# Mixture-of-experts loop: rows sorted once ahead of it, 32 rows always and 64 more if needed, narrow and wide jobs in turn

## The reference, cut to what matters

```python
def grouped_moe(x, w_router, router_bias, w_gate, w_up, w_down):
    scores = jax.nn.sigmoid((x @ w_router).astype(jnp.float32))
    sel = scores + router_bias.astype(jnp.float32)
    ...                       # one group of four experts, then its two best
    combine = ...             # normalised gates, 0 for experts not chosen
    y = jnp.zeros_like(x)
    for e in range(N_EXPERTS):
        h = jax.nn.silu(x @ w_gate[e]) * (x @ w_up[e])
        y = y + combine[..., e:e + 1] * (h @ w_down[e])
    return y
```

## Time and profile before

| what | value |
|---|---|
| median of 3 runs (lowest, highest) | 1649.84 us (1643.22, 1656.58) |
| the profiled execution, its own time | 1639.89 us |
| its span in the trace | 1637.9 us |
| mean granted TensorE clock | 0.971 of 2.4 GHz |
| PE busy | 1497.6 us (91%) |
| DVE, ACT, POOL busy | 435.7, 253.6, 160.7 us |
| bytes moved | 558.64 MB, 341 GB/s over the span |

### The profile page before, as it was taken

The page is one execution under the profiler, slowest core; times in us unless marked ns, Lnnn a source line. Parts: engine busy times, 40 slices in busy tenths (PEclk is TensorE's granted clock), DMA queues, the critical chain, the costliest instruction groups (busy, mean ns, idle before and its releaser), DMA issues.

```text
span 1637.9 us, 18866 instructions
## 1 busy us (share of the span) xinstructions
PE 1497.6 (91%) x7398; PEld 678.2 (41%) x7399; DVE 435.7 (27%) x765; ACT 253.6 (15%) x546; POOL 160.7 (10%) x157
## 2 busy tenths in 40 slices
PE   4899936998999889999899998999999999999995
PEld 3566413554445424434244342443434434434442
DVE  3103947776560402010220102201022012011014
ACT  3001031232100122101121011210112102102201
POOL 0101983121220000000000000000000000000001
PEclk9999967999999999999999999999999999999998
DMA  9998245776795699997799976999789999999993
GB/s 385 404 377 322 73 171 181 267 263 252 279 363 212 245 398 421 421 403 290 282 421 422 406 289 266 423 422 413 294 325 422 422 422 422 422 422 422 422 422 155
DMA packets 84335, 558.64 MB, mean 341 GB/s; under 512 B 9728, under 2 KB 9728, under 8 KB 22720
## 3 DMA queue, kind: packets, MB, share of 16 engines
q1 hardware_dynamic: 69408, 501.99, 75.7%
q0 software_dynamic: 14304, 51.76, 8.6%
q10 hardware_dynamic: 576, 4.19, 0.6%
HBM read 555.81 MB, written 2.10 MB: 341 GB/s over the span
## 4 chain that ended last, share of the span: by engine, by line
PE 74%; DMA 12%; POOL 5%; DVE 3%; ACT 2%; issue 2%; ACTq 0%; DVEq 0%; POOLq 0%
PE ps L761 21%; PE ps L786 14%; DMA ring<-w_up_dram 8%; PE ps L739 8%; PE ps L802 7%; PE ps L661 7%; POOL halves L433 5%; PE ps L558 4%; PE ps L552 3%; PE ps L766 3%; DMA ring<-w_half_dram 2%; PE ps L790 1%; PE ps L469 1%; DMA tokens<-ctx_dram 1%; DVE halves L1070 1%
## 5 line engine op out<-in xcount | busy, mean ns | idle before, releaser
L761 PE MATMUL ps<-ring,nT_all 128*64 128x512 f32 x2048 | 466.9, 605 | 26.7 <-issue 13.4
L761 PEld LDWEIGHTS ps<-ring,nT_all 128*64 128x64 f32 x2048 | 140.4, 138 | 330.4 <-issue 287.5
L786 PE MATMUL ps<-ring,bufA 128*64 128x512 f32 x1024 | 227.9, 596 | 0.0
L558 PE MATMUL ps<-ring,nT_all 128*128 128x512 f32 x320 | 149.5, 610 | 17.2 <-ACT early L899 17.2
L1387 DVE TENSOR_TENSOR work<-work,ps 128x512 f32<-128x512 f32 x16 | 11.0, 687 | 505.9 <-PE ps L761 375.3
L786 PEld LDWEIGHTS ps<-ring,bufA 128*64 128x64 f32 x1024 | 70.3, 137 | 144.1 <-issue 142.6
L739 PEld LDWEIGHTS ps<-bufB,tokens 128*128 128x128 f32 x1088 | 124.0, 192 | 12.9 <-issue 11.8
L739 PE MATMUL ps<-bufB,tokens 128*128 128x96 f32 x1088 | 127.7, 276 | 0.2 <-DVE bufB L1372 0.2
L802 PE MATMUL ps<-nT_all 64*128 64x512 f32 (+1 forms) x256 | 114.1, 596 | 12.7 <-ACT nT_all L321 12.7
L1070 DVE SCALAR_TENSOR_TENSOR halves<-ring,silu_c,halves 128x1024 f32<-128x1024 f32 x82 | 105.2, 1283 | 65.5 <-DMA ring<-w_half_dram 31.9
L447 POOL TENSOR_TENSOR nT_all<-nT_all,early 128x1024 f32<-128x1024 f32 x1 | 3.2, 3242 | 1111.1 <-DVE small L1415 1111.1
(11 more groups left out here) (273 smaller groups left out, 947.8 us busy)
## 6 DMA issues: line engine op xcount, KB each, us to landing
ring<-w_gate_dram SPq DMA_DIRECT2D x128, 1024.0 KB, 12.0
ring<-w_up_dram SPq DMA_DIRECT2D x128, 1024.0 KB, 9.5
ring<-w_down_dram SPq DMA_DIRECT2D x128, 1024.0 KB, 15.7
ring<-w_half_dram POOLq DMA_DIRECT2D x96, 512.0 KB, 5.7
ring<-w_mix_dram SPq DMA_DIRECT2D x32, 1024.0 KB, 11.0
ring<-w_in_dram SPq DMA_DIRECT2D x28, 1024.0 KB, 7.5
ring<-w_out_dram SPq DMA_DIRECT2D x16, 1024.0 KB, 6.3
ring<-w_gmod_dram SPq DMA_DIRECT2D x16, 1024.0 KB, 5.9
```

What stands on the lines that cost most here:

```text
L558: mm = pe.matmul(ps[:, b + t, :], nT[:, k, t * P:(t + 1) * P], w, start=(k == 0), stop=(k == KT - 1))
L761: mm = pe.matmul(out_b[0][BASE * f:BASE * (f + 1), :], xg[:, k, 0:BASE], w[:, kk, f * N:(f + 1) * N], start=(k == 0), stop=(k == KT - 1))
L786: mm = pe.matmul(Db[0][BASE * (q // 2):BASE * (q // 2 + 1), q % 2, :], hT[0][:, (i % 4) * P + BASE * (i // 4):(i % 4) * P + BASE * (i // 4 ...
```

## The change

1. Sorting ahead of the loop. DVE works out a place among 512 for each pair (all experts' rows one behind the other) and builds a 256 x 512 one-hot matrix. PE multiplies it with all 16 column tiles of the tokens (new steps "gather" k, 128x512 each, two matmuls per k), ACT writes the result to xg_all. The three last routing steps and the four "gate_b" steps (formerly L818) are threaded between them. Inside the loop, PE's gathers, DVE's gather_matrix and ACT's save_tokens are gone; ACT copies the next job's rows out of xg_all at a register's offset (job_rows).
2. BASE, REST = 32, 64: 32 rows always (32 columns of the array, four quarters side by side), 64 more rows if the job is wide (64 columns, two halves). With the counts above seven jobs are wide (91, 69, 88, 33, 35, 36, 51).
3. Scatter in row groups: the 32 rows of each quarter of the outputs stand on their own 32 partitions (outs[0] is 128x512), so the four scatter matmuls use four different row groups of the array. The 64 rows use two.
4. Order: narrow and wide in turn. Here N W seven times, then N N.
5. The constants grow by 720 columns; y's memset moves behind POOL's last loads.

```diff
-BASE, REST = 64, 32
+BASE, REST = 32, 64
...
-    seq += [("hT", 3)] + gate[8:9] + [("logits", 3)] + gate[9:13] + [("route", 1)] + gate[13:14]
-    return seq + [("route", 2)] + gate[14:15] + [("route", 3)] + gate[15:16]
+    seq += [("hT", 3)] + gate[8:9] + [("logits", 3)] + gate[9:13] + [("route", 1)] + gate[13:16]
+    for k in range(KT):
+        seq.append(("gather", k))
+        if k in (0, 2, 5):
+            seq.append(("route", 2 + (0, 2, 5).index(k)))
+        seq += [("gate_b", (k - 8) // 2)] * (k >= 8 and k % 2 == 0)
...
-            pool.wait_ge(slot_free, used(U_))
-            pool.memset(nT_all[:, 0:TT * D], 0.0).then_inc(y_zeroed, 1)
...
+            pool.wait_ge(logit_done, 1)
+            pool.memset(nT_all[:, TT * D + P:2 * TT * D + P], 0.0).then_inc(y_zeroed, 1)
...
+                elif kind == "gather":
+                    k = step[1]
+                    if k == 0:
+                        pe.wait_ge(oh_ready, 1)
+                    elif k > 1:
+                        pe.wait_ge(sorted_saved, k - 1)
                     for t in range(TT):
+                        mm = pe.matmul(S[k % 2], tokens[:, t, k * P:(k + 1) * P], oh_all[:, t, :],
                                        start=(t == 0), stop=(t == TT - 1))
+                    mm.then_inc(gathered, 1)
...
-                            for f in range(2):
+                            for f in range(4):
                                 mm = pe.matmul(out_b[0][BASE * f:BASE * (f + 1), :], xg[:, k, 0:BASE],
-                                               w[:, kk, f * N:(f + 1) * N], start=(k == 0), stop=(k == KT - 1))
+                                               w[:, kk, f * 256:(f + 1) * 256], start=(k == 0), stop=(k == KT - 1))
                         for kk in range(2 * wide):
                             k = 2 * i + kk
-                            for f in range(4):
+                            for f in range(2):
                                 mm = pe.matmul(out_b[1][REST * f:REST * (f + 1), :], xg[:, k, BASE:BLK],
-                                               w[:, kk, f * 256:(f + 1) * 256], start=(k == 0), stop=(k == KT - 1))
+                                               w[:, kk, f * N:(f + 1) * N], start=(k == 0), stop=(k == KT - 1))
-                pe.wait_ge(oh_ready, j + 2)
-                pe.wait_ge(summed, j * 4 + 4)
-                gather(0)
...
-                gather(1)
...
-                pe.wait_ge(xg_ready, j + 2)
-                rows_used = BLK if wide else BASE
+                pe.wait_ge(o_act, j + 1)
+                pe.wait_ge(summed, j * 4 + 4)
                 for t in range(TT):
                     for q in range(4):
-                        if t == 0:
-                            pe.wait_ge(o_dve if q % 2 else o_act, j * 2 + (q // 2 + 1))
-                        elif q % 2 == 0:
+                        if t == 1 and q % 2 == 0:
                             pe.wait_ge(summed, j * 4 + (5 + q // 2))
-                        mm = pe.matmul(Yb[:, q, :], spread_T[0:rows_used, t, :],
-                                       outs[0:rows_used, q * N:(q + 1) * N], start=True, stop=True)
+                        mm = pe.matmul(Yb[:, q, :], spread_T[0][BASE * q:BASE * (q + 1), t, :],
+                                       outs[0][BASE * q:BASE * (q + 1), :], start=True, stop=not wide)
+                        if not wide and q % 2:
+                            mm.then_inc(scattered, 1)
+                    if wide and t == 0:
+                        pe.wait_ge(o_dve, j + 1)
+                    for q in (0, 2, 1, 3) if wide else ():
+                        mm = pe.matmul(Yb[:, q, :], spread_T[1][REST * (q // 2):REST * (q // 2 + 1), t, :],
+                                       outs[1][REST * (q // 2):REST * (q // 2 + 1), q % 2, :], start=False, stop=True)
                         if q % 2:
                             mm.then_inc(scattered, 1)
...
+            def job_rows(at):
+                span = big[:, bass.ds(at + SORTED, KT * 2 * SEQ)].rearrange("p (k s) -> p k s", k=KT)
+                return copy(xg, span[:, :, 0:BLK]).then_inc(xg_ready, 1)
...
+            for t in range(TT):
+                ts(oh_all[:, t, :], k_("slots"), place4[:, 0, t:t + 1], rs_tok[:, t:t + 1], ALU.is_equal, ALU.mult)
+                last = ts(oh_more[:, t, :], k_("slots"), place4[:, 1, t:t + 1], rs_tok[:, t:t + 1],
+                          ALU.is_equal, ALU.mult)
+            link(last)
+            tt(oh_all, oh_all, oh_more, ALU.add).then_inc(oh_ready, 1)
...
-                save_outputs(dve, nc.vector.tensor_copy, 1, wide)
+                if wide:
+                    nc.vector.tensor_copy(outs[1], Db[1]).then_inc(o_dve, 1)
```

More of the change, by code:

```diff
@@ L373, in _ @@
             sp.wait_ge(table_ready, 1)
[L374 removed]
+            jobs = sp.value_load(n_i[0:1, 3 * JOBS:3 * JOBS + 1], min_val=1, max_val=JOBS - 1)
             with sp.Fori(0, jobs) as j:
@@ L807, in _ @@
             pe.wait_ge(table_ready, 1)
[L808 to L817, removed]
-                pe.matmul(C[i % 2], k_("spread")[:, i * P:(i + 1) * P], modrow[:, 0, :], start=True, stop=True) \
-                    .then_inc(bcast_done, 1)
+            jobs = pe.value_load(n_i[0:1, 3 * JOBS:3 * JOBS + 1], min_val=1, max_val=JOBS - 1)
             with pe.Fori(0, jobs) as j:
@@ L982, in _, with job_evac @@
             act.activation(rt[:, 1], rt[:, 0], ACT.Sigmoid).then_inc(score_saved, 1)
-            act.wait_ge(table_ready, 1)
-            jobs = act.value_load(n_i[0:1, 2 * JOBS:2 * JOBS + 1], min_val=1, max_val=JOBS - 1)
-            def save_tokens(half):
-                for k in range(8 * half, 8 * half + 8):
-                    last = act.activation(xg[:, k, :], Xb[:, k // 4, (k % 4) * BLK:(k % 4 + 1) * BLK], ACT.Identity,
-                                          bias=modcol[:, 3, k, 0:1], scale=scale_ffn[:, k:k + 1])
-                return last
-            def job_evac(j, wide):
+            act.wait_ge(gate_done, 1)
+            copy(modrow[:, 0, :], C[1]).then_inc(gate_saved, 1)
+            for k in range(KT):
+                act.wait_ge(gathered, k + 1)
+                act.activation(xg_all[:, k, :], S[k % 2], ACT.Identity, bias=modcol[:, 3, k, 0:1],
+                               scale=scale_ffn[:, k:k + 1]).then_inc(sorted_saved, 1)
+                if k >= 9 and k % 2:
+                    i = (k - 9) // 2
+                    act.wait_ge(bcast_done, 5 + i)
+                    copy(gate_b[:, i * N:(i + 1) * N], C[i % 2]).then_inc(bcast_saved, 1)
+            act.wait_ge(table_ready, 1)
+            jobs = act.value_load(n_i[0:1, 3 * JOBS:3 * JOBS + 1], min_val=1, max_val=JOBS - 1)
+            def job_rows(at):
+                span = big[:, bass.ds(at + SORTED, KT * 2 * SEQ)].rearrange("p (k s) -> p k s", k=KT)
+                return copy(xg, span[:, :, 0:BLK]).then_inc(xg_ready, 1)
+            def job_evac(j, wide, at):
                 act.wait_ge(slot_free, j * JCH + used_job(7))
@@ L1341, in _ @@
             dve.wait_ge(order_done, 1)
-            col = [vcol[:, i:i + 1] for i in range(8)]
+            col = [vcol[:, i:i + 1] for i in range(8)] + [vcol[:, 9:10]]
+            tt(col[8], T[0:CAND, 4:5], k_("blk_lo")[0:CAND, :], ALU.add)
             link(nc.vector.tensor_copy(vcol[:, 2:6], T[0:CAND, 0:4]))
@@ L1383, in hidden_product @@
             def hidden_product(j, wide):
+                for i in range(1 + wide):
+                    spread_matrix(j, i)
                 dve.wait_ge(silu_saved, j + 1)
@@ L1389, in hidden_product @@
                 dve.wait_ge(ehT_done, j + 1)
[L1390 to L1391 removed]
+                for i in range(1 + wide):
+                    last = nc.vector.tensor_copy(spread_T[i].rearrange("p t n -> p (t n)"), Ub[i][:, 0:SEQ])
+                last.then_inc(spread_saved, 1)
                 dve.wait_ge(slot_free, j * JCH + used_job(23))
[L1393 to L1396 removed]
+                if wide:
+                    nc.vector.tensor_copy(outs[1], Db[1]).then_inc(o_dve, 1)
+                else:
+                    ts(small[:, 34:35], small[:, 63:64], 1.0, None, ALU.mult).then_inc(o_dve, 1)
+            jobs = dve.value_load(n_i[0:1, 3 * JOBS:3 * JOBS + 1], min_val=1, max_val=JOBS - 1)
+            dve.wait_ge(gathered, KT)
             dve.wait_ge(y_zeroed, 1)
```

183 lines of the change are left out of this document (88 added, 95 removed).

## The result

The changed kernel takes 1742.72 us (median of 4 runs, 1742.40 to 1744.62), against 1653.21 us for the kernel before in the same comparison: ratio 1.055, 95% interval 1.050 to 1.061. It is slower, as forecast, but by 5.5% instead of 1.4%, and outside the range (1628 to 1712). The profiled execution took 1742.40 us, with a span of 1740.5 us and a mean granted clock of 0.887 (0.971 before).

A forecast was written before the change was run, and what follows sets the result against it. The weight stream bounds narrow jobs, TensorE wide ones. PE's start at 604.7, first narrow job, seven pairs of 132.6 us, last narrow job and tail gave a 1660.3 us span, scaled to 1672 us; range 1628 to 1712.

The forecast's parts named there:

- The loop's start: Ahead of the loop: after the longer sort, PE starts the loop at 604.7 us instead of 585.24.
- Chunks and bridge: In the jobs: narrow chunks 1.00 us, wide chunks 2.86, up-to-down bridge 3.7, a wide job's down part 22.9.
- The model of the ring: Eight-slot weight ring: wide jobs are not hidden, leaving it empty of work for 10.1 us in each narrow-wide pair.
- Narrow to wide shows no gap in three of three: Job switches: narrow to wide costs nothing; wide to narrow has a mean gap of 2.5 us.
- rival E: Wide job's start: half clock or a gap, 20 us over seven jobs, median near 1693; chance 0.14.
- the wide tail: End of a wide job: copy, scatter passes, sums and waits take 8.2 us.
- the narrow tail: End of a narrow job: from the last chunk's landing through copy, sums and scatter, 5.6 us.
- the restart of the stream: Weight stream after a wide job: reload lands 4.9 us after issue, then fifteen chunks take 37.3 us.
- B: Job switches: no switch cost, every pair at 129.4 us, about 1650 as a median; chance 0.22.
- C: Wide jobs: they fit into the ring and the stream never stops, at its end a median of 1579; chance 0.13.
- D: Scatter: row groups do not run side by side, a median near 1742; chance 0.09.
- F: Job counts: if rounding moved pair counts 33 to 32, six jobs would be wide, 13 us less; inside the range.

The follow-up runs named there:

- Straight code: The changed kernel with PE's 16 jobs written out one behind the other, without loop or branch on PE; 1690.50 us, ratio 1.025 to the kernel before.
- dead code: 160 never-executed matmuls added to PE's loop in the kernel that takes only the sort from the change; 1684.58 us, against 1633.31 without them.
- the two orders: The changed kernel's alternating order, 1742.72 us, and the same kernel with N N W four times, then N W W W, 1734.72 us.
- the sort alone: Only the change's sort ahead of the loop, with the old job sizes, scatter and order, against the kernel before; 1633.31 us, ratio 0.992.
- late extra work: Changed kernel with PE's jobs written out, plus idle matmuls behind up chunks 2 to 7 and down chunks 0 to 6 of narrow jobs; 1681.32 us, ratio 1.016.

## Why the prediction was wrong

- *The loop's start* came at 605.09 for 604.7, by errors that nearly cancel, which is luck: the sort began 2.6 us late, against which stand the 0.9 us added for the larger table and an entry 1.0 us shorter (4.7 for 5.76).
- *Chunks and bridge* were right: 1.00 to 1.07 us narrow, 2.87 wide, 3.45 us from up to down (3.7 forecast), 23.0 us for down (22.9).
- *The model of the ring* was right: each wide job stops the stream, so every us on PE's path between a narrow job's landing and the freed slot counts sevenfold. That is why small misses became 80 us of span.
- *"Narrow to wide shows no gap in three of three"* is the step that failed first. It took the two gaps of the earlier trace rows as a price of a kind of switch and carried it over to another loop body. Straight code and dead code show that the gap is a fetch of code, and the two orders that it depends on which part ran before. It measured 5.3 to 6.0 us, in each pair but the first, at the switch that I had priced at zero; the one that I had priced at 2.5 us had it once in seven. How far the loop's size and how far the order of the bodies sets it stays open.
- *The clock* is the second. I had seen the risk as rival E, gave it 0.14, and dismissed it by one stretch at 46 us where PE was busy for 0.68 of 2 us at full clock. In the loop the clock did fall at the end of narrow jobs (781.57 and 784.05 above). In the pair of the table it costs 1.9 us in the narrow tail and 2.5 us at the wide start, nearly as much as the gap (over the six pairs 1.9 and 2.3 on the mean). Rival E had the mechanism; its 1693 lacked the tail and the gap, since it said "half clock, or a gap" where both came.
- *Terms that were mis-sized:* the wide tail 9.3 for 8.2, the narrow tail 0.9 us without its half clock, and the restart of the stream 1.6 us. The traffic between 745 and 775 us, in 40 slices of 0.75 us, shows the restart:

```profile
GB/s 0 0 0 120 218 426 393 328 186 262 415 404 393 415 404 437 426 426 437 415 448 426 415 415 426 437 404 426 415 448 426 404 415 415 448 415 426 415 404 448
```

The first load is issued at 746.50. Two slices at 120 and 218 GB/s follow, two at 426 and 393, and then three more at 328, 186 and 262 before the stream stays near 420. These seven slices move 1.45 MB where 422 GB/s would move 2.2, an estimate of 1.8 us lost. I had counted the latency and then full rate at once. No run tried to remove this.
- *The other rivals.* B (no switch cost) and C (the ring hides the wide jobs) fell; the version without wide jobs shows where C's end would have been, 1568.5 against 1579. D had the right time, 1742 us, with a wrong mechanism: the row groups take 0.14 us a pass. F fell: seven jobs are wide. A total that agrees proves no mechanism.
- *Which part of the change costs.* The sort ahead of the loop gains 0.8% alone. The rest, 32 rows instead of 64 with the new scatter and the alternating order, turns three wide jobs into seven and costs the difference, 109 us by the medians and 104 by the ratios; of these parts only the order was tested by itself. The loop's form is 52 us of it. Of the 80 us of span that the forecast missed, seven pairs of the table make 70: the clock 31, the gaps net of what I had counted 14, tails 14, the restart 11. Straight code has no gap at any switch, as rival B had it, and still takes 1690 us where B said 1650: these 40 us are what is left for the clock, the tails and the restart. The part of the clock is read from rows; the late extra work removed some of it (9 to 15 us), no run all of it.

## What to carry to other kernels

A loop with two bodies is longer than what either job executes. Count its instructions, read the packets of the instruction queue, and look at which body runs behind which: here the count grew by 2% and the gaps behind "issue" went from two to eight, so neither the old kernel's switches nor the count alone would have told it. In this kernel, speeding up the jobs that wait for a transfer made none of them shorter (59.6 us each, in the kernel before and in the version without wide jobs), and it left the engine idle enough to lose its clock just before the job where the engine is the bound. Before filling such idle time, see whether it is the time in which the engine catches up.

## What was not expected of the hardware

- 160 matmuls that are never executed, in a loop of 16 rounds, cost 51 us: four gaps of 12.6 to 12.9 us appeared, each with four instruction packets in it, and one of 5.8 with one packet.
- The gap does not come at each round: 3.07 us once in the sort alone, and in the changed kernel 5.3 to 6.0 us at the end of each narrow job between a wide one and another job.
- The granted clock fell from 2.4 to 1.2 GHz at 784 us, after a stretch of bursts of 1.06 us with waits of 1.42 us, and stayed at 1.00 at 1184 to 1192 us in the version with late extra work, with PE busy for 5.77 of 8 us; it fell there at 1194 us, behind the scatter and its waits.
- Four matmuls of 32 rows in four row groups ran at 0.14 us a pass, three times as fast as one of full height (0.431).
